# Interleaving the last two weight groups of four MLP stages with each other and with the next stage's first transposes

## What is computed

```python
def _sqrelu_mlp(x, w_up, w_down):
    return jnp.square(jax.nn.relu(x @ w_up)) @ w_down
...
x = _layernorm(DEEPNORM_ALPHA * x + _sqrelu_mlp(x, ffn_w_up[i], ffn_w_down[i]), ln_ffn_g[i], ln_ffn_b[i])
...
def rmsnorm(x, g):
    xf = x.astype(jnp.float32)
    y = xf * lax.rsqrt(jnp.mean(xf * xf, axis=-1, keepdims=True) + EPS)
    return (y * g.astype(jnp.float32)).astype(x.dtype)
```

## Time and profile before

| | us |
|---|---|
| median of 3 runs | 2669.77 |
| lowest, highest | 2665.67, 2673.15 |
| the profiled execution, its own time | 2667.0 |
| its span in the trace | 2665.2 |
| TensorE busy in it | 2582.8 |
| VectorE, ScalarE, GpSimd busy | 1021.8, 857.4, 1048.5 |
| mean granted clock of TensorE | 0.982 of full speed |

### The profile page before, as it was taken

One profiled execution on the slowest core, in us unless ns is written; L12 is line 12 of the kernel. 1 busy time (PEld: TensorE's weight loads), 2 busy tenths in 40 slices (PEclk: granted clock), 3 DMA queues, 4 the chain that ended last, 5 costly groups with the idle time before them and its releaser, 6 DMA issues.

```text
span 2665.2 us, 32424 instructions
## 1 busy us (share of the span) xinstructions
PE 2582.8 (97%) x12149; PEld 2114.4 (79%) x12149; DVE 1021.8 (38%) x1854; ACT 857.4 (32%) x1224; POOL 1048.5 (39%) x824
## 2 busy tenths in 40 slices
PE   8998999999997999998999999999999999999998
PEld 6667888888886888888887788888877876888887
DVE  4456444456665444445222422223322132322224
ACT  4334322234555322223323422222322322322222
POOL 4122444444331444443233244444334333344443
PEclk9899999999998999997999999999999999999999
DMA  5112333322211323332121222222322222232222
GB/s 165 50 48 68 95 95 100 103 79 96 80 64 32 111 95 99 103 97 75 48 79 64 75 97 97 94 94 95 119 72 87 81 78 79 77 106 95 94 94 79
DMA packets 161317, 230.40 MB, mean 86 GB/s; under 512 B 10886, under 2 KB 127628, under 8 KB 161100
## 3 DMA queue, kind: packets, MB, share of 16 engines
q1 hardware_dynamic: 161228, 229.17, 26.6%
HBM read 227.06 MB, written 2.10 MB: 86 GB/s over the span
## 4 chain that ended last, share of the span: by engine, by line
PE 89%; DVE 4%; issue 4%; ACT 2%; POOL 1%; DMA 0%; SPq 0%; DVEq 0%; POOLq 0%; ACTq 0%
PE bank L586 13%; PE bank L588 13%; PE bank L587 13%; PE bank L599 9%; PE bank L597 9%; PE bank L598 9%; PE bank L1130 2%; PE bank L1131 2%; PE bank L1132 2%; PE bank L768 2%; PE bank L1156 1%; PE bank L732 1%; PE bank L713 1%; PE bank L788 1%; PE bank L644 1%
## 5 line engine op out<-in xcount | busy, mean ns | idle before, releaser
L560 POOL TENSOR_TENSOR w_lo<-w_raw,w_hi 128x512 fp32r<-128x512 f32 (+1 forms) x820 | 1048.3, 1310 | 1596.1 <-ACT w_hi L1229 1596.1
L1229 ACT ACTIVATE w_hi<-w_raw 128x2048 fp32r<-128x2048 f32 (+1 forms) x205 | 392.2, 1913 | 713.5 <-PE bank L599 429.3
L586 PE MATMUL bank<-h_hi,w_hi 128*128 128x512 f32 x1520 | 597.0, 393 | 3.2 <-DVE x_residual L1727 1.2
L587 PE MATMUL bank<-h_lo,w_hi 128*128 128x512 f32 x1520 | 592.9, 390 | 0.0
L588 PE MATMUL bank<-h_hi,w_lo 128*128 128x512 f32 x1520 | 592.8, 390 | 0.0
L1727 DVE TENSOR_TENSOR x_residual<-x_residual,bank 128x512 f32<-128x512 f32 x496 | 338.4, 687 | 411.5 <-PE bank L599 386.8
L597 PE MATMUL bank<-w_hi,act_hi 128*128 128x512 f32 x992 | 386.6, 390 | 1.4 <-DVE act_lo L2148 1.4
L599 PE MATMUL bank<-w_hi,act_lo 128*128 128x512 f32 x992 | 386.4, 390 | 0.0
L598 PE MATMUL bank<-w_lo,act_hi 128*128 128x512 f32 x992 | 386.4, 389 | 0.0
L586 PEld LDWEIGHTS bank<-h_hi,w_hi 128*128 128x128 f32 x1520 | 286.3, 188 | 68.0 <-issue 9.1
L587 PEld LDWEIGHTS bank<-h_lo,w_hi 128*128 128x128 f32 x1520 | 286.4, 188 | 59.5 <-issue 0.7
(11 more groups left out here) (220 smaller groups left out, 2971.0 us busy)
## 6 DMA issues: line engine op xcount, KB each, us to landing
w_raw<-in_ffn_w_in SPq DMA_DIRECT2D x44, 1024.0 KB, 5.1
w_raw<-in_ffn_w_up SPq DMA_DIRECT2D x32, 1024.0 KB, 5.5
w_raw<-in_ffn_w_down SPq DMA_DIRECT2D x32, 1024.0 KB, 5.0
w_raw<-in_ret_w_in SPq DMA_DIRECT2D x24, 1024.0 KB, 5.2
w_raw<-in_ffn_w_out SPq DMA_DIRECT2D x22, 1024.0 KB, 4.9
w_raw<-in_diff_w_qkv SPq DMA_DIRECT2D x12, 1024.0 KB, 5.2
w_raw<-in_fox_w_in SPq DMA_DIRECT2D x12, 1024.0 KB, 5.4
w_raw<-in_ret_w_out SPq DMA_DIRECT2D x8, 1024.0 KB, 5.0
```

Source lines behind the costliest of these rows:

```text
L560: last = nc.gpsimd.tensor_tensor(m.w_lo[:, sl, at], m.w_raw[:, sl, at], m.w_hi[:, sl, at].bitcast(F32), ALU.subtract)
L586: mm(out, hi, x[0][:, k, :], start=k == 0, stop=False)
L587: mm(out, hi, x[1][:, k, :], start=False, stop=False)
L1229: m.nc.scalar.activation(m.w_hi[:, sl, 0:width], m.w_raw[:, sl, 0:width], ACT.Copy).then_inc(m.sem("w_hi_ready"), 1)
```

## The change

In ffn0, ffn1, sw0 and sw1 the 16 down blocks of the last two groups are made in another order: blocks 0 to 3 of the last group but one, blocks 0 to 3 of the last, then 4 to 7 of the one and 4 to 7 of the other. Banks are 4 to 7, 0 to 3, 0 to 3, 0 to 3. In ffn0, ffn1 and sw0 the first half of the next stage's transposes stands ahead of the last two blocks (`beside`); in sw1 nothing stands there. The last group's weights are thereby wanted four blocks earlier, and all uses of the last group but one end four blocks later. VectorE adds blocks 4 to 7 of the last group but one (`held`) between the norm's steps for tiles 0 and 1. ScalarE's split of the next stage's first unit moves out of the MLP's function to behind the deviations of tiles 0 and 1. The two loops of the squared-ReLU stages run 6 rounds in place of 7, with the rest unrolled. The diff, cut (the unchanged logic of `rows_complete` and `halves_complete`, which only rename counts, is left out):

```diff
+TAIL = [(0, n) for n in range(4)] + [(1, n) for n in range(4)] + [(0, n) for n in range(4, 8)] + [(1, n) for n in range(4, 8)]
+TAIL_BANK = {x: (4, 5, 6, 7, 0, 1, 2, 3, 0, 1, 2, 3, 0, 1, 2, 3)[n] for n, x in enumerate(TAIL)}
+TAIL_COUNT = {x: n + 1 for n, x in enumerate(TAIL)}
+def tiles_complete(groups):
+    return [KC * (groups - 2) + TAIL_COUNT[1, 2 * tile + 1] for tile in range(TT)]
...
+    def last_two(names):
+        for which, n in TAIL:
+            done(names[which], n)
...
+def pe_last_groups(m, pe, t, groups, beside):
+
+    names = [f"{t}.d{groups - 2}", f"{t}.d{groups - 1}"]
+    base = KC * (groups - 2)
+    for which, n in TAIL:
+        at = 2 * ((groups - 2 + which) % 2)
+        if n == 0:
+            pe_weights(m, pe, [names[which]])
+            pe.wait_ge(*m.upto(f"{t}_a_lo", 2 * (groups - 1 + which)))
+        if (which, n) == (1, 6):
+            beside()
+        if n >= 4:
+            pe.wait_ge(*m.upto(f"{t}_acc", base + TAIL_COUNT[which, n] - 4))
+        elif which == 0:
+            pe.wait_ge(*m.upto(f"{t}_acc", base + n - 3))
+        pe_tokens(m, m.bank[TAIL_BANK[which, n]][:, :], weight(m, [names[which]], 2048, 2),
+                  (m.act_hi[:, at:at + 2, :], m.act_lo[:, at:at + 2, :]), 2, n // 2, 512, 512 * (n % 2)).then_inc(m.sem("blocks_done"), 1)
...
 def pe_relu_mlp
-    with pe.Fori(0, (G1 - 2) // 2) as i:
+    with pe.Fori(0, (G1 - 4) // 2) as i:
...
-    down([G1 - 1])
+    up([G1 - 2])
+    down([G1 - 3])
+    up([G1 - 1])
+    pe_last_groups(m, pe, t, G1, beside)
...
 def pe_swiglu
-    down([G2 - 2])
-    down([G2 - 1])
+    pe_last_groups(m, pe, t, G2, beside)
...
 def act_layernorm
-    deviation(0), deviation(1), scale(0), scale(1), deviation(2)
+    deviation(0), deviation(1), scale(0), scale(1)
+    if first:
+        act_split(m, act, [first])
+    deviation(2)
     act_high(m, act, to, 0)
...
 def act_rms
-    scale(0), scale(1), scale(2)
+    scale(0), scale(1)
+    if first:
+        act_split(m, act, [first])
+    scale(2)
     act_high(m, act, t, 0)
...
 def act_relu_mlp
-    down([G1 - 1])
+    up([G1 - 2]), down([G1 - 3])
+    up([G1 - 1]), down([G1 - 2])
 def act_swiglu
     gate([G2 - 1]), up([G2 - 1]), down([G2 - 2])
-    down([G2 - 1])
...
 def dve_layernorm
-    center(0), center(1), finish(0), finish(1), scale(0), scale(1), center(2)
+    center(0), center(1), held(0), finish(0), held(1), finish(1), scale(0), scale(1), held(2), held(3), center(2)
 def dve_rms
-    add(0), add(1), scale(0), scale(1), add(2)
+    add(0), add(1), scale(0), held(0), held(1), scale(1), held(2), held(3), add(2)
 def dve_end
-    add(0), add(1), scale(0), add(2), scale(1), add(3), scale(2), scale(3)
+    add(0), add(1), scale(0), held(0), held(1), scale(1), held(2), held(3), add(2), scale(2), add(3), scale(3)
...
+def dve_last_groups(m, dve, t, groups, sums):
+    base = KC * (groups - 2)
+    def adder(which):
+        def add(n):
+            before = base + TAIL_COUNT[0, n] if which else base - KC + n + 1
+            dve_add_block(m, dve, t, n, m.bank[TAIL_BANK[which, n]], [f"{t}.d{groups - 2 + which}"], n, None, None, False, sums and which == 1, before)
+        return add
+    return adder(0), adder(1)
...
+    def last_groups():
+        adds = dve_last_groups(m, dve, t, G1, True)
+        for n in range(4):
+            adds[0](n)
+        end(adds[1], tiles_complete(G1), lambda n: adds[0](4 + n))
```

More of the change, by code:

```diff
@@ L158, in relu_mlp @@
             if g:
-                unit(f"{t}.d{g - 1}"), done(f"{t}.d{g - 1}", *range(KC))
+                unit(f"{t}.d{g - 1}")
+            if 0 < g < G1 - 1:
+                done(f"{t}.d{g - 1}", *range(KC))
+        last_two([f"{t}.d{G1 - 2}", f"{t}.d{G1 - 1}"])
     def pairs(t):
@@ L175, in swiglu @@
             if g:
-                unit(f"{t}.d{g - 1}"), done(f"{t}.d{g - 1}", *range(KC))
+                unit(f"{t}.d{g - 1}")
+            if 0 < g < G2 - 1:
+                done(f"{t}.d{g - 1}", *range(KC))
+        last_two([f"{t}.d{G2 - 2}", f"{t}.d{G2 - 1}"])
     relu_mlp("ffn0")
@@ L617, in pe_first_blocks, with pe_input_turn, pe_input @@
                 last.then_inc(m.sem("blocks_done"), 1)
-def pe_input(m, pe, t, made, source, added, count, unit):
+def pe_input_turn(m, pe, t, made, source, half):
+    s, b, nc = m.sem, m.bank, m.nc
+    pe.wait_ge(*m.upto(made, 2 * half + 2))
+    if half:
+        pe.wait_ge(*m.upto(f"{t}_h_lo", 4))
+    for j in range(4):
+        for k in (2 * j, 2 * j + 1):
+            for tile in (2 * half, 2 * half + 1):
+                at = 256 * (k % 2) + P * (tile % 2)
+                last = nc.tensor.transpose(b[4 + j][:, at:at + P], source(tile)[:, k * P:(k + 1) * P], m.ident)
+        last.then_inc(s(f"{t}_h_turned"), 1)
+def pe_input(m, pe, t, made, source, added, count, unit, turned=False):
     s, b, nc = m.sem, m.bank, m.nc
@@ L624, in pe_input @@
     for half in range(2):
[L625 to L633, removed]
+        if half or not turned:
+            pe_input_turn(m, pe, t, made, source, half)
         pe_weights(m, pe, [unit])
@@ L1293, in act_std, with act_layernorm @@
     run(m.x_std[:, tile:tile + 1], m.x_sq[:, tile:tile + 1], ACT.Sqrt, scale=1 / D, bias=m.eps[:, eps:eps + 1]).then_inc(s(f"{t}_std"), 1)
-def act_layernorm(m, act, t, to, second):
+def act_layernorm(m, act, t, to, first, second):
     def deviation(tile):
@@ L1313, in act_layernorm, with act_rms @@
     act_high(m, act, to, 1)
-def act_rms(m, act, t, added, count, per_tile, second):
+def act_rms(m, act, t, added, complete, first, second):
     def scale(tile):
-        act.wait_ge(*m.upto(added, count + per_tile(tile)))
+        act.wait_ge(*m.upto(added, complete[tile]))
         act_std(m, act, t, tile, 1)
-    scale(0), scale(1), scale(2)
+    scale(0), scale(1)
+    if first:
+        act_split(m, act, [first])
+    scale(2)
     act_high(m, act, t, 0)
@@ L1521, in down @@
     def down(gs, i=None):
-        if not (last and gs[-1] == G2 - 1):
-            act_split(m, act, after([f"{t}.d{g}" for g in gs]), i)
+        act_split(m, act, after([f"{t}.d{g}" for g in gs]), i)
     gate([0]), up([0])
@@ L1711, in residual_block, with dve_add_block @@
     return m.x[:, tile, 512 * half:512 * half + 512]
-def dve_add_block(m, dve, t, n, bank, names, part, i, steps, first, sums=False):
+def dve_add_block(m, dve, t, n, bank, names, part, i, steps, first, sums=False, before=None):
     s, v = m.sem, m.nc.vector
@@ L1719, in dve_add_block @@
     if not first:
-        dve.wait_ge(*m.upto(f"{t}_acc", along(i, [KC * (g - 1) + n + 1 for g in steps])))
+        dve.wait_ge(*m.upto(f"{t}_acc", before or along(i, [KC * (g - 1) + n + 1 for g in steps])))
     if sums:
@@ L1750, in dve_rms_tile, with dve_layernorm @@
         .then_inc(s(f"{t}_normed"), 1)
-def dve_layernorm(m, dve, add, added, count, t, rows, to):
+def dve_layernorm(m, dve, add, added, complete, t, rows, to, held):
     s, v = m.sem, m.nc.vector
@@ L1758, in center @@
         add(2 * tile), add(2 * tile + 1)
-        dve.wait_ge(*m.upto(added, count + 2 * tile + 2))
+        dve.wait_ge(*m.upto(added, complete[tile]))
         at = slice(2 * tile, 2 * tile + 1), slice(2 * tile + 1, 2 * tile + 2)
@@ L1784, in dve_layernorm, with dve_rms @@
     dve_low(m, dve, to, 1)
-def dve_rms(m, dve, add, t, rows):
+def dve_rms(m, dve, add, t, rows, held):
     def scale(tile):
         dve_rms_tile(m, dve, t, tile, m.normed[:, tile % 2, :], rows)
-    add(0), add(1), scale(0), scale(1), add(2)
+    add(0), add(1), scale(0), held(0), held(1), scale(1), held(2), held(3), add(2)
     dve_low(m, dve, t, 0)
@@ L1952, in attend_last @@
         head_low(c)
-        end(lambda n: added(p, n, t in POST_NORMED), KC * (PAIRS - 1))
+        end(lambda n: added(p, n, t in POST_NORMED), rows_complete(PAIRS), lambda n: None)
     project_first()
@@ L2038, in dve_relu_mlp @@
     down([0])
-    with dve.Fori(0, (G1 - 2) // 2) as i:
+    with dve.Fori(0, (G1 - 4) // 2) as i:
         for e in range(2):
-            up(range(2 + e, G1, 2), i)
-            down(range(1 + e, G1 - 1, 2), i)
-    end(adder([G1 - 1]), KC * (G1 - 1))
+            up(range(2 + e, G1 - 2, 2), i)
+            down(range(1 + e, G1 - 3, 2), i)
+    up([G1 - 2])
+    down([G1 - 3])
+    up([G1 - 1])
+    last_groups()
 def dve_swiglu(m, dve, t, end):
@@ L2060, in up, with last_groups @@
                 .then_inc(s(f"{t}_a_lo"), 1)
[L2062 to L2066, removed]
     def down(gs, i=None):
         for n in range(KC):
-            adder(gs, i)(n)
+            dve_add_block(m, dve, t, n, b[4 + n % 4], [f"{t}.d{g}" for g in gs], n, i, gs, gs[0] == 0)
+    def last_groups():
+        adds = dve_last_groups(m, dve, t, G2, False)
+        for n in range(4):
+            adds[0](n)
+        end(adds[1], lambda n: adds[0](4 + n))
     up([0]), up([1]), down([0])
@@ L2196, in dve_program @@
```

(4 more changed lines are left out.)

85 lines of the change are left out of this document (40 added, 45 removed).

## The result

| | before | changed |
|---|---|---|
| median, us | 2669.71 (18 runs) | 2675.72 (18 runs) |
| lowest to highest | 2665.67 to 2673.15 | 2670.52 to 2678.07 |
| ratio of the changed kernel | | 1.0022, 95% interval 1.0016 to 1.0028 |
| span of the profiled execution | 2665.2 | 2668.7 |

The change makes the kernel 6.0 us slower, with an interval of some 4.3 to 7.5. That is clear of noise for so many runs, and inside the 0.3% that the prediction took as the bound of "same". The profiled execution is the fastest of the changed kernel's 18, so the two spans differ by less than the medians do.

A forecast was written before the change was run, and what follows sets the result against it. TensorE, busy for 2582.8 of 2665.2 us, was taken to bound the kernel. Stage terms of plus 4.8 us and clock falls of plus 5.1 made plus 9.9, on the median of 2669.8 giving 2679.7, range 2671 to 2687.

The forecast's parts named there:

- part 1: Last group in all four stages: TensorE waits for w_lo 2.8, 2.8, 3.0 and 3.0 us, together 11.6 us new idle time.
- part 2: Norm chain after the stalls: minus 0.8 us at ffn0, minus 0.7 at ffn1; with sw0 and sw1, plus 4.8 in all.
- the prediction's rival: Last group's weights come in time, TensorE never stalls, and the interleave gives minus 6.8 us, 2663; chance 0.12.
- sw0: At sw0 into ret the norm chain was not the limit; the second transposes come 1.7 us later.
- sw1: At the kernel's end TensorE ends 3.0 us later, VectorE's order adds 1.5 to 1.7: together plus 4.6.
- part 3: TensorE's clock halves behind three of the four stalls, each costing 1.7 us: plus 5.1; fox's present half clock stays.
- The unrolled code at nothing: The unrolled rounds cost nothing, as TensorE has no idle time at its loop turns.
- The next unit's weights: ffn0: last blocks end at 602.4, next unit's weights come at 602 to 603, under the earlier 603.15, so neither decides.
- the likeliest case: Whole kernel: stalls with two to four clock falls, 2679.7 us, slower; chance 0.47.
- few falls of the clock: Rival: none, one or, at the edge, two clock falls behind the stalls; plus 4.8 to 7 us, 2676; chance 0.31.
- the upper bounds: Highest stage sums: plus 0.6 us on ffn0's and ffn1's norm chains if both copies take 1.97; 5.2 at sw1.

The follow-up runs named there:

- Run 1: Changed kernel, but blocks 0 to 3 of the last group use the previous group's ready weights, output not the reference's: 2656.03 us, ratio 0.9954 to the kernel before.
- run 4: Changed kernel, but at the very end VectorE adds blocks 6 and 7 ahead of tile 2's norm: 2673.85 us, ratio 1.0014 to the kernel before.
- run 2: Changed kernel with the new order in ffn0 and ffn1 only, sw0 and sw1 as before: 2667.70 us, ratio 0.9992 to the kernel before.
- run 3: Changed kernel with the new order in sw0 and sw1 only, ffn0 and ffn1 as before: 2679.10 us, ratio 1.0038 to the kernel before.
- run 7: Changed kernel's shorter loops and unrolled rounds, with the old block order in all four stages: 2667.85 us, ratio 1.0000 to the kernel before.
- run 5: Changed kernel, but six blocks ahead of the last group's first in ffn0, ffn1 and sw0, sw1 as before: 2662.89 us, ratio 0.9980 to the kernel before.
- run 6: Changed kernel, but five blocks ahead of the last group's first in ffn0, ffn1 and sw0, sw1 as before: 2662.17 us, ratio 0.9974 to the kernel before.
- run 8: Changed kernel, but five blocks ahead in ffn0 and ffn1, six in sw0, sw1 as before: 2661.79 us, ratio 0.9971 to the kernel before.

## Why the prediction was right, and where it was off

- **The stalls** (part 1): forecast 2.8, 2.8, 3.0 and 3.0 us; measured 2.78, 2.78, 2.88 and 2.88, shown in the waits on line 590. The prediction has ffn1 611.8 us behind ffn0 where its two rows are 621.8 apart; the stall doesn't hang on it. Run 1 shows that the stalls, with what follows them, are the cause: 20 us lie between the change and the same order without them.
- **The norm chain in ffn0 and ffn1** (part 2): forecast minus 0.8 and minus 0.7 without a fall, plus 0.9 and 1.0 with one. Measured plus 0.4 with one at ffn0; minus 0.9 and minus 1.1 without, plus 0.9 with one, at ffn1. The copies of tiles 0 and 1 at 1.28 us were as forecast. The copy of tile 2 was forecast nearer by under 1 us: so it was only without a fall (1.3 nearer in run 4 at ffn1); in the change, with the falls, it came 0.4 and 0.2 later. At ffn0 with a fall it came 0.5 us better than forecast. In run 1, 4.3 against the 3.6 of the prediction's rival.
- **sw0**: forecast plus 1.7 and plus 3.4 with a fall; measured 1.7 and 3.3.
- **sw1**: forecast 3.0 for the stall, 1.5 to 1.7 for VectorE's order, 1.7 for a fall: 6.3 together. Measured 6.3 to the last norm, of which 1.5 by run 4.
- **The clock** (part 3): three of four falls were taken; over the profiles of the change and of runs 2, 3 and 4 it fell behind 8 of 12 such stalls. That is two thirds in place of three quarters; by place it was 3 of 3 at ffn0, 1 of 3 at ffn1, 1 of 3 at sw0 and 3 of 3 at sw1. The rows' ten of eleven would have been too high. What failed is the rest of the term: it adds new falls and keeps all the old ones ("the half clock seen now at fox's transposes stays"). It did not stay: the first of these transposes took 1.97 us in place of 3.67. The granted clock, recorded with every execution, has a mean of 0.9820 over the 18 of the change, and of 0.9806, 0.9811 and 0.9813 over 21, 26 and 13 of the kernel before. By these, as an estimate, TensorE ran at half clock for 96 us with the change and for 100 to 103 before: on the whole less, not more.
- **The unrolled code at nothing**: run 7. **The next unit's weights**: the step that says neither the last blocks' end nor the weights decide was wrong in detail. With the fall, the split moved later with the eighth block, and TensorE waited for it 0.95 us at 605.15 and 1.62 at 1228.22. It cost at most 0.1 us at the second transposes of diff and nothing at those of fox, since VectorE's chain set these.

The time: forecast 2679.7 in 2671 to 2687, measured 2675.72. The sign, the places and most sizes were right. The term that was mis-sized is the clock, part 3. Behind the stalls themselves plus 5.1 was nearly right: the table and two thirds of falls give 4.5 to 4.7. But with the measured terms (minus 1.3, minus 1.0, 1.7, 4.5) the sum is 8.5, and the measured difference 6.0. The 2.5 us between, 1 to 4 by the interval, lie outside the changed stretches, and the recorded clocks point to where: other falls became rarer. It is the same in the faster runs, which gained 2 to 5 us more than their stretches show: their mean clocks are 0.9854 (run 1), 0.9829 (5), 0.9834 (6) and 0.9839 (8). With the new order in ffn0 and ffn1 alone it is 0.9828, in sw0 and sw1 alone 0.9790. How much of a half clock decides the end, and why falls elsewhere become rarer, no run shows. So the likeliest case, slower by over 8 us, did not come. What came was its mechanism, stalls with three falls in the profile, at the time of the case "few falls of the clock" (2676, 0.31), which isn't what happened behind the stalls; that it ended inside the range is in part luck. The top of that range was also set too high: four falls and the upper bounds add up to 2685, not 2687.

The Trainium skill, TensorE: Matmul & The Clock Gate, Part 1, says that what watches TensorE's activity runs free of the kernel. The traces agree at ffn1, where the same stall of 2.78 us had the half clock behind it in the change, and not in runs 2 and 4; at ffn0 and sw1 it fell all three times, and three times are too few to tell this from chance.

## What to carry to other kernels

When work is pulled ahead to hide a latency, ask first when its inputs come: here weights that were there 2.4 to 2.6 us ahead of their use in the old order came 2.8 to 3.0 us late in the new one, and no engine's busy share showed it. Pulling it ahead only by what its inputs allow (behind five or six blocks in place of four), together with the old order at the end of the program, turned a loss of 6 us into a gain of 6 to 7. Interleaving pays only where a latency is behind it: at the end of the program there is no next stage, and even without the stall (run 1) TensorE gained nothing there and the last norm came 1.5 us later. And before a term for the clock is added to a sum, the falls that the old kernel has must be in it too, since they move when the work around them moves.

## What the runs showed that was not expected

- GpSimd's split beside VectorE's instructions with two SBUF inputs lengthens these from 1.28 us to up to 2.10, so that moving a split by 4 us (599.09 against 594.88) can undo what a shorter queue saves. But the same copy beside a split can also take 1.28. A split is four pieces, and in these traces the instruction ends 1.08 us behind the end of the piece that ran when it started:

| run, place | piece of the split | VectorE's instruction starts | takes |
|---|---|---|---|
| 5, ffn0 | 594.88 to 596.15 | 595.13 | 2.10 |
| the change, ffn0 | 600.33 to 601.63 | 600.74 | 1.97 |
| 6, ffn0 | 597.16 to 598.44 | 598.14 | 1.38 |
| the change, ffn1 | 1223.41 to 1224.71 | 1224.51 | 1.28 |

The split's next piece then takes 2.3 us in place of 1.3. It looks as if the two took turns; what was measured is the times, and no run was made to test it.

- Stalls of TensorE between dense work are followed by half clock in only part of the cases: 8 of 12 at 2.8 to 2.9 us, and none of 5 at 1.5 (three in run 6, two in run 8).
